# A block of two model parts on one core: where the chunk table's two loads stand among the eight lag-table loads

## The reference, cut to what matters

```python
u = h.reshape(bsz, seqlen, SSM_GROUPS, SSM_GROUP)        # 64 groups of 16 channels
# per group: state_t = Abar state_{t-1} + Bbar u_t, 64 complex states
bu_re = einsum('blgh,gph->blgp', u, bbar_re)             # and bu_im
_, _, xr, xi = lax.associative_scan(_ssm_combine, (a_r, a_i, bu_re, bu_im), axis=1)
y = einsum('ghp,blgp->blgh', c_re, xr) - einsum('ghp,blgp->blgh', c_im, xi)
y = gelu(y + d * h)
val, gate = split(y @ w_out, 2)                          # the GLU projection
mix = val * sigmoid(gate)
```

## Time and profile before

| | |
|---|---|
| median of three runs | 2602.72 us (2601.14 to 2610.35) |
| the profiled execution | 2603.56 us |
| its span | 2601.8 us |
| PE busy | 2537.4 us (98%) |
| DVE busy | 1939.6 us (75%) |
| ACT busy | 1352.5 us (52%) |
| POOL busy | 217.6 us (8%) |
| experts' share of the chain that ended last, L2564 alone | 39% |

### The profile page before, as it was taken

The page is one execution under the profiler, slowest core; times in us unless marked ns, Lnnn a source line. Parts: engine busy times, 40 slices in busy tenths (PEclk is TensorE's granted clock), DMA queues, the critical chain, the costliest instruction groups (busy, mean ns, idle before and its releaser), DMA issues.

```text
span 2601.8 us, 34375 instructions
## 1 busy us (share of the span) xinstructions
PE 2537.4 (98%) x12258; PEld 2077.5 (80%) x12258; DVE 1939.6 (75%) x1837; ACT 1352.5 (52%) x1364; POOL 217.6 (8%) x321
## 2 busy tenths in 40 slices
PE   9999999999999999999998989999999999999998
PEld 7777788888888888888886468888888888888886
DVE  7878999999999999999999787788633445433422
ACT  5333777777777777777775353322222223222222
POOL 2150100000000000000000401111000000000000
PEclk9999999999999999999999999999999999999999
DMA  9545999999999999999995957377433631233432
GB/s 326 210 107 194 326 412 409 389 386 386 385 385 382 391 378 390 387 384 384 389 382 212 198 121 219 123 243 241 143 105 89 162 97 32 65 97 97 109 89 77
DMA packets 351758, 643.92 MB, mean 247 GB/s; under 512 B 27152, under 2 KB 220560, under 8 KB 350928
## 3 DMA queue, kind: packets, MB, share of 16 engines
q1 hardware_dynamic: 327600, 540.83, 60.8%
q0 software_dynamic: 17872, 78.13, 8.4%
q10 hardware_dynamic: 6224, 24.12, 2.3%
HBM read 616.87 MB, written 26.16 MB: 247 GB/s over the span
## 4 chain that ended last, share of the span: by engine, by line
PE 71%; issue 15%; DVE 8%; DMA 4%; SPq 1%; ACT 1%; POOL 0%; ACTq 0%; POOLq 0%; DVEq 0%
PE bank L2564 39%; PE bank L2830 8%; PE bank L2838 8%; PE bank L2831 8%; SPq L554 1%; PE bank L2552 1%; PE bank L2540 1%; PE bank L2547 1%; DMA ring<-k_dram 1%; DMA ring<-in_w_in 1%; DVE slot_lo L1871 1%; PE bank L2358 1%; DVE rows L1973 1%; PE bank L2387 1%; PE bank L2389 1%
## 5 line engine op out<-in xcount | busy, mean ns | idle before, releaser
L1871 DVE TENSOR_TENSOR slot_lo<-ring,slot_hi 128x2048 fp32r<-128x2048 f32 x384 | 863.6, 2284 | 69.0 <-ACT slot_hi L1072 68.8
L1072 ACT ACTIVATE slot_hi<-ring 128x2048 fp32r<-128x2048 f32 x384 | 736.4, 1920 | 253.7 <-PE bank L2564 226.6
L2564 PE MATMUL bank<-slot_hi,xs_hi 128*128 128x512 f32 x1024 | 316.1, 390 | 0.3 <-issue 0.3
L2564 PE MATMUL bank<-slot_hi,xs_lo 128*128 128x512 f32 x1024 | 315.6, 389 | 0.0
L2830 PE MATMUL bank<-h_hi,fin_hi 128*128 128x512 f32 x704 | 274.1, 389 | 0.8 <-DVE fin_lo L2146 0.7
L2564 PE MATMUL bank<-slot_lo,xs_hi 128*128 128x512 f32 x1024 | 274.3, 390 | 0.5 <-DVE slot_lo L1871 0.4
L2831 PE MATMUL bank<-h_hi,fin_lo 128*128 128x512 f32 x704 | 273.9, 389 | 0.0
L2564 PEld LDWEIGHTS bank<-slot_lo,xs_hi 128*128 128x128 f32 x1024 | 192.1, 188 | 41.5 <-DVE slot_lo L1871 1.3
L2564 PEld LDWEIGHTS bank<-slot_hi,xs_lo 128*128 128x128 f32 x1024 | 192.2, 188 | 40.8
L2564 PEld LDWEIGHTS bank<-slot_hi,xs_hi 128*128 128x128 f32 x1024 | 192.1, 188 | 40.8 <-issue 0.7
L2146 DVE TENSOR_TENSOR fin_lo<-rows,fin_hi 128x1024 fp32r<-128x1024 f32 x88 | 103.7, 1221 | 127.7 <-ACT fin_hi L1341 127.7
(11 more groups left out here) (480 smaller groups left out, 3988.9 us busy)
## 6 DMA issues: line engine op xcount, KB each, us to landing
ring<-in_expert_w_gate_up SPq DMA_DIRECT2D x256, 1024.0 KB, 7.1
ring<-in_expert_w_down SPq DMA_DIRECT2D x128, 1024.0 KB, 6.7
rows<-in_w_ffn_in SPq DMA_DIRECT2D x88, 512.0 KB, 5.0
work<-in_w_ada POOLq DMA_DIRECT2D x64, 384.0 KB, 4.2
y_dram<-cb ACTq DMA_DIRECT2D x32, 512.0 KB, 7.1
ring<-in_w_ada POOLq DMA_DIRECT2D x36, 384.0 KB, 5.2
work<-in_w_ffn_out SPq DMA_DIRECT2D x8, 1408.0 KB, 7.0
rows<-in_w_ffn_out SPq DMA_DIRECT2D x8, 1408.0 KB, 7.0
```

Source lines behind the costliest of these rows:

```text
L1072: act.activation(hi_of(e, j), slot[q], ACT.Copy).then_inc(s_slot_hi, 1)
L1871: tt(slot_lo[:, q], slot[q], whole(hi_of(e, j)), ALU.subtract).then_inc(s_slot_lo, 1)
L2564: last = mm(ps[banks + n], x[:, k, :], (lo if lower else hi)[:, k, 512 * n:512 * (n + 1)], start=(begins and lower == 0 and k == 0 and x i ...
```

## The change

SP issues lags 0 to 5, then both halves of the chunk table, then lags 6 and 7. The halves count on a semaphore of their own, `s_mw_in`; the first half no longer waits for any lag load. The chunk sums wait on that semaphore, and the first `input_rows` gets a wait for all eight lag loads.

```diff
+        s_mw_in = sem("mw_in")
...
             sp.wait_ge(s_k_out, 16 * (CH + 1))
-            for v in range(CH):
-                load(m_t[GC * v:GC * (v + 1), :, :], kd[:, :, (CH - 1 - v) * GC:(2 * CH - 1 - v) * GC], s_t_in)
+
+            def load_lags(first, end):
+                for v in range(first, end):
+                    load(m_t[GC * v:GC * (v + 1), :, :], kd[:, :, (CH - 1 - v) * GC:(2 * CH - 1 - v) * GC], s_t_in)
+
+            load_lags(0, 6)
             for half in range(2):
                 sp.wait_ge(s_pgate_ready, 2 * NT - 1 + half)
-                sp.wait_ge(s_t_in, 16 * (CH + half))
+                if half:
+                    sp.wait_ge(s_mw_in, 16)
                 load(m_w[:, GP * half:GP * (half + 1), :],
-                     m_w_dram.rearrange("p (g m) -> p g m", g=G)[:, GP * half:GP * (half + 1), :], s_t_in)
+                     m_w_dram.rearrange("p (g m) -> p g m", g=G)[:, GP * half:GP * (half + 1), :], s_mw_in)
+            load_lags(6, CH)
...
                 if b % 2 == 0:
-                    pe.wait_ge(s_t_in, 16 * (CH + 1 + b // 2))
+                    pe.wait_ge(s_mw_in, 16 * (b // 2 + 1))
...
             def input_rows(k):
+                if k == 0:
+                    pe.wait_ge(s_t_in, 16 * CH)
                 if k < 2:
                     pe.wait_ge(s_x_state, 1)
```

## The result

The changed kernel takes 2609.36 us (median of 22 runs, 2606.12 to 2614.87) against 2606.39 us for the kernel before (22 runs beside it). The ratio is 1.0014, 95% interval 1.0008 to 1.002. The change makes the kernel about 3 us slower, where 1.7 us of gain was forecast. The predicted range was 2598.8 to 2605.0 us. The 22 runs also put the kernel before at 2606.39 us, 3.7 us above the median of its first three and itself above that range, so a part of the miss is that the three runs were low. The wrong sign is not: it is read from the ratio to runs made side by side.

The account below looks back on a forecast made before the run. Bound: lag loads delaying the chunk table's first half and so the chunk sums, then VectorE's recurrences. The one term, 1.70 us, came off the 2602.72 us median, giving 2601.0; 8-in-10 range 2598.8 to 2605.0 us.

Parts of the forecast that it names:

- The first step: At the chunk sums: the first half of the chunk table lands earlier, so the sums start 1.70 us earlier.
- More than 1.70: At the chunk sums: a larger gain was called excluded, since nothing before 1520.66 uses either table.
- The new wait ahead of the rows of outputs: PE's wait on the lag count before the output rows: one instruction, under 0.1 us.
- Lags 6 and 7, moved past both halves: On SP's queue: they land at about 1531.5, before their first reader at 1541.2.
- cover of 9.7 us: Time between lags 6 and 7 landing, about 1531.5, and their first reader in the new order, 1541.2.
- PE's instructions arrive late under lags 6 and 7: Rival at chunk sums and u columns, 1520.8 to 1531.5: slower, +1.7 us, 2604.4; chance 0.08 including late lags.
- the worse of the two: At the instruction fetch in the chunk sums: large packets, as before, could delay it more than a fuller queue.
- 3.66 us of added idle in three pieces: The slower rival's price: the 1.22 us issue idle doubled, plus one more under each of two lag loads.
- Does the 1.70 us survive?: Behind the chunk sums: VectorE's and TensorE's lines both shift whole, so the 1.70 us gain is kept.
- The two tight lines: VectorE's recurrences, without a gap, and TensorE's output rows, 0.24 us to spare; both must shift with the chunk sums.
- slack of 0.24: Spare us in TensorE's output rows: the first 29 need 2.74 us in the third pair, 2.98 in the fourth.

Follow-up runs that it names:

- e10: e9 plus five unused 256-column matmuls in TensorE's gap before x_columns(1); ratio 0.9987 to the kernel before.
- e4: Changed kernel with lags 6 and 7 replaced in place by two loads of the same bytes in 4 KB runs; ratio 0.9988 to the kernel before.
- e6: Changed kernel with lags 0 to 3 ahead of the halves and lags 4 to 7 behind them; 2617.56 us, ratio 1.0041 to the kernel before.
- e7: Changed kernel plus five unused 256-column matmuls (20 instructions) in TensorE's gap before x_columns(1); ratio 1.0007 to the kernel before.
- e9: Changed kernel with three lag loads issued 12 us earlier, the other five also ahead of both halves; 2604.43 us, ratio 0.9988 to the kernel before.
- e1: Changed kernel without the loads of lags 6 and 7; ratio 0.9994 to the kernel before.
- e8: Changed kernel reordered to lags 0 to 6, first half, lag 7, second half; ratio 0.999 to the kernel before.
- e2: Changed kernel with all eight lag loads ahead of both halves, the chunk table keeping its own semaphore; ratio 0.9993 to the kernel before.
- e3: Changed kernel reordered to lags 0 to 5, first half, lags 6 and 7, second half; ratio 0.9989 to the kernel before.
- e5: Changed kernel run again with no edit, on another day's chip; ratio 1.001 to the kernel before.

## Why the prediction was wrong

**The first step held.** The first half was issued at 1502.21, landed before the second half's issue at 1512.5, and the sums no longer waited for it. They started 1.78 us earlier; 1.70 was forecast. More than 1.70 was called excluded, wrongly: the copy L2066 was taken as fixed at 9.73 us after x_columns(0), but it starts at 9.38 in e10, and the sums start at 10.17 or 10.18 in e4, e6, e7, e9 and e10, 2.1 earlier than before. The new wait ahead of the rows of outputs cost nothing, as forecast: the lag loads were through by 1530, and these rows start at 1547.69 without an idle before them.

**The step that failed** is "Lags 6 and 7, moved past both halves", with its cover of 9.7 us. I asked who reads those two loads and found L2787, which indeed never waited for them. The traffic itself had another user. It stood in the list of rivals, "PE's instructions arrive late under lags 6 and 7", as the main part of a case at 0.08, and its sign, an issue idle of over 2 us between 1520 and 1532, came. What it cost is the 2.87 us of idle and 1.59 us of lower clock of the sum above. e1 shows that it is that traffic, e7 that the idle sits at the end of an instruction block, and e6 and e8 that it grows with the traffic.

**Why its chance was put too low.** I wrote that a queue with large packets "could by it be the worse of the two". The rows spoke against this already: DMA share 1.26 under lag loads and 0.66 under a half, though 0.66 is a mean over a stretch in which the half passed for 6 of 8.6 us; from 1523 to 1529 it was 0.93. The rival named the place, 1520.8 to 1531.5, and its pace, 64 matmuls and 64 weight loads in 2.08 us, but I did not count back: 256 instructions before the split of the kernel before lies matmul 37 of chunk_sums(0), the same boundary one block earlier. There the kernel before had no idle, and nothing fuller than the first half was in flight.

**What the rival itself missed.** It priced 3.66 us of added idle in three pieces. It was one of 2.87 plus 1.59 us of halved clock, which no term of mine had. The Trainium skill's rule that an engine changes queues only at a packet's end ("DMA: Bandwidth & Descriptors", Queues, rings and completion order) agrees with a fetch delayed by full engines; the packet's own time also doubled, 0.96 to 2.14 us, which that rule does not give. The doubling could account for 1.2 of the 2.87 us.

**"Does the 1.70 us survive?"** The two tight lines were read rightly. e7 delays only TensorE's line and loses 67.32 - 63.20 = 4.1 us of the 4.41 of idle; the 0.3 us that it does not lose fits the slack of 0.24.

**Open.** The instruction packets carry no engine's name in the view, so that the one at 1523 is TensorE's is inferred from its time. The traces bear it out: in all nine issue idles inside the chunk sums (before, changed, e2, e3, e5, e6 twice, e7, e8) TensorE goes on 1.3 to 1.9 us after the end of such a packet. They also show most of the wait. On empty engines the next packet starts 0.2 to 0.3 us after TensorE has entered a block, that is after the first matmul behind the split (e1, e4, e9); under the second half 3.9 and 3.7 us after (before, e2), and under lag loads 6.2 and 11.9 us after (e7, e6). What the fetch waits for in that time is not shown. And the times of e3 and e8 disagree with their profiles.

## What to carry to other kernels

When a load is moved, ask what runs while it passes, and not only who reads it: code that spends 64 matmuls and 64 weight loads in 2 us needs a new block of 256 instructions every 4 us, over the same DMA engines. Loads in short runs fill these engines for long at few bytes (about 10 us for 1 MB here), so put them beside slow instructions, and keep the stretches of many short matmuls free. An idle marked issue that always splits a loop at the same matmul is the end of a block; count 256 instructions from it to find the others before you move traffic.

## What the hardware showed that I had not expected

- A block that is asked for under a full DMA load can come over 8 us late: 4.05 and 8.13 us of idle in e6, none in e1, e4 and e9, where the engines were empty by then.
- An idle of 2.87 us in the middle of work at the full clock was followed by about 3 us at 1.2 GHz, although TensorE had worked again for a microsecond when the clock fell. The 1.22 us of the kernel before and the 1.37 of e8 were not.
- 20 instructions put into a gap changed the stretch from 68.2 to 67.3 us with the same traffic and moved the idle by a whole block.
